# Causal mask and position bias added by VectorE inside the row maximum, in place of matmuls into the score bank

## The reference, cut to what matters

```
s_own = einsum('hqd,hld->hql', qi, k_own) * scale + table_t[:, rel_bucket(d_own)]
s_own = where(d_own[None] >= 0, s_own, -inf)
p = softmax(concatenate([s_sel, s_own], axis=-1))
```

## Time and profile before

| | before |
|---|---|
| median of three runs | 1194.9 us |
| profiled execution, first to last instruction | 1194.0 us |
| PE / DVE / ACT busy | 1178.5 / 742.4 / 623.6 us |
| score matmuls L1185 + L1189 | 96 + 96, of 128 to 512 columns |
| mask matmuls L1197 | 64 |
| bias matmuls L1494 | 64 |
| row maxima L2393 | 112, of them 96 in the three causal loops |

### The profile page before, as it was taken

How to read it: one execution, slowest core, us unless ns; L and a number is a source line. 1 busy time by engine, 2 the same in 40 slices (tenths; PEclk the granted TensorE clock), 3 DMA queues, 4 the chain that set the end, 5 groups by cost and what they waited for, 6 DMA issues and landing times.

```text
span 1194.0 us, 16132 instructions
## 1 busy us (share of the span) xinstructions
PE 1178.5 (99%) x6034; PEld 984.1 (82%) x6034; DVE 742.4 (62%) x1123; ACT 623.6 (52%) x1054; POOL 158.6 (13%) x255
## 2 busy tenths in 40 slices
PE   9999999999999999999999999999999999999997
PEld 7788887778888888888788898888898888888886
DVE  6667576755333475674387775455647659558478
ACT  5566785685332255532676554352455445464464
POOL 3233223410000021000133000010001010000010
PEclk9999999999999999999999999999999999999999
DMA  6422233113443543342112545221286553743732
GB/s 198 108 58 66 71 91 103 37 54 106 106 105 105 176 132 102 106 142 71 36 54 106 162 139 165 71 101 51 73 247 141 172 130 87 227 108 91 210 71 88
DMA packets 152139, 133.37 MB, mean 112 GB/s; under 512 B 5553, under 2 KB 124401, under 8 KB 152066
## 3 DMA queue, kind: packets, MB, share of 16 engines
q1 hardware_dynamic: 144688, 113.13, 31.6%
q0 software_dynamic: 4000, 13.67, 5.9%
q10 hardware_dynamic: 3378, 5.60, 1.5%
HBM read 115.55 MB, written 4.22 MB: 100 GB/s over the span
## 4 chain that ended last, share of the span: by engine, by line
PE 90%; DVE 5%; ACT 2%; DMA 1%; issue 1%; POOL 0%; DVEq 0%; ACTq 0%; POOLq 0%
PE lin L993 23%; PE lin L995 23%; PE lin L994 23%; PE tr L1175 2%; PE sc L994 2%; PE sc L995 2%; PE sc L993 2%; PE sc L1189 1%; PE sc L1185 1%; PE tr L1168 1%; PE tr L994 1%; PE tr L993 1%; PE tr L995 1%; DVE w_lo L2368 1%; PE lin L1213 1%
## 5 line engine op out<-in xcount | busy, mean ns | idle before, releaser
L993 PE MATMUL lin<-h_hi,w_hi 128*128 128x512 f32 (+1 forms) x824 | 318.0, 386 | 0.0
L995 PE MATMUL lin<-h_hi,w_lo 128*128 128x512 f32 (+1 forms) x824 | 310.5, 377 | 0.0
L994 PE MATMUL lin<-h_lo,w_hi 128*128 128x512 f32 (+1 forms) x824 | 310.4, 377 | 0.0
L2368 DVE TENSOR_TENSOR w_lo<-w_raw,w_hi 128x1024 fp32r<-128x1024 f32 x160 | 196.6, 1232 | 140.8 <-ACT w_hi L1637 139.7
L1637 ACT ACTIVATE w_hi<-w_raw 128x1024 fp32r<-128x1024 f32 x162 | 170.8, 1056 | 145.0 <-PE lin L995 48.6
L995 PEld LDWEIGHTS lin<-h_hi,w_lo 128*128 128x128 f32 x824 | 155.7, 189 | 28.5
L993 PEld LDWEIGHTS lin<-h_hi,w_hi 128*128 128x128 f32 x824 | 155.8, 189 | 27.2 <-issue 0.6
L994 PEld LDWEIGHTS lin<-h_lo,w_hi 128*128 128x128 f32 x824 | 156.1, 189 | 24.5
L2393 DVE TENSOR_REDUCE neg_max<-sc 128x1 f32<-128x128 f32 (+3 forms) x112 | 52.4, 478 | 55.4 <-PE sc L1189 35.5
L2368 DVE TENSOR_TENSOR u_lo<-u_raw,u_hi 128x256 fp32r<-128x256 f32 (+2 forms) x48 | 37.4, 779 | 68.6 <-ACT u_hi L2252 37.4
L993 PE MATMUL lin<-w_hi,h_hi 128*128 128x512 f32 x160 | 63.4, 397 | 0.0
(11 more groups left out here) (399 smaller groups left out, 2356.6 us busy)
## 6 DMA issues: line engine op xcount, KB each, us to landing
w_raw<-in_w_in SPq DMA_DIRECT2D x74, 512.0 KB, 3.9
w_raw<-in_w_up SPq DMA_DIRECT2D x32, 512.0 KB, 4.4
wd_b<-in_w_down SPq DMA_DIRECT2D x24, 512.0 KB, 5.3
w_raw<-in_w_out SPq DMA_DIRECT2D x16, 512.0 KB, 3.6
w_raw<-in_w_xkv SPq DMA_DIRECT2D x16, 512.0 KB, 3.9
x_m<-in_x SPq DMA_DIRECT2D x8, 512.0 KB, 5.6
w_raw<-in_w_branch SPq DMA_DIRECT2D x8, 512.0 KB, 4.2
w_raw<-in_w_xq SPq DMA_DIRECT2D x8, 512.0 KB, 3.9
```

Source lines behind the costliest of these rows:

```text
L993: pe.matmul(o, lh, rh, start=start, stop=False)
L994: pe.matmul(o, lh, rl, start=False, stop=False)
L995: return pe.matmul(o, ll, rh, start=False, stop=stop)
L2368: return dve.tensor_tensor(out, x, as_f32(hi), ALU.subtract)
```

## The change

For the 96 score tiles of fox, diff and moba, the mask and bias matmuls are gone. In place of the row maximum stands one `tensor_tensor_reduce` on DVE (`biased_max`): it reads the score bank and a bias tile in SBUF, writes -(score + bias) back over the bank, and takes the minimum of that, which is the negated maximum. The exponential reads the bank with scale -1. In fox and diff the bias tile is `bias_c`, zero with -1e30 above the diagonal in its last 128 columns, made by POOL behind the roots of the first norm; in moba there is one tile of 128x512 for each head. The bias rows are no longer split: 8 rows of 640 entries are written to memory 128 times each (8 x 128 x 640 floats, 2.6 MB, from 8 partitions), and read back with a row step of 639 entries into 8 tiles of 128x512 (2.1 MB, as many bytes as before). DVE, and no longer PE, waits for them. The warm-up matmuls at the start read ones in place of `ident_b` and `future_b`. The row maxima of "x" stay as they were.

```diff
+BIAS_ROW = 640
...
-             ("g_x", [P, 2, T], F32), ("beta", [P, BIAS_COLS], F32), ("one_hot", [P, BIAS_COLS], F32),
-             ("beta_hi", [P, BIAS_COLS], F32R), ("beta_lo", [P, BIAS_COLS], F32R), ("beta_0", [P, 1], F32)],
+             ("g_x", [P, 2, T], F32), ("beta", [P, BIAS_ROW], F32), ("one_hot", [P, BIAS_COLS], F32),
+             ("beta_0", [P, 1], F32)],
...
-            [("pad_z", [P, 34 * T], F32), ("bias_b", [P, 4 * 256], F32R)])
+            [("pad_z", [P, 34 * T], F32), ("bias_b", [P, 2 * T], F32)])
...
-            [("pad_b", [P, 4 * PT_COLS + P_COLS], F32), ("bias_a", [P, 9 * 256], F32R)],
+            [("pad_b", [P, 4 * PT_COLS + P_COLS], F32), ("bias_a", [P, 4 * T], F32)],
...
-        flip = sb("flip", [P, P], F32R)
...
-        bias_c = sb("bias_c", [P, 256], F32R)
-        ident_b = sb("ident_b", [P, P], BF16)
-        future_b = sb("future_b", [P, P], BF16)
+        bias_c = sb("bias_c", [P, T], F32)
...
-        bias_places = [B["bias_a"][:, :], B["bias_b"][:, :], c_row[:, :], bias_c[:, :]]
-        bias_16 = [place[:, 256 * n:256 * n + 256] for place in bias_places for n in range(place.shape[1] // 256)]
+        bias_places = [B["bias_a"][:, :], B["bias_b"][:, :], as_f32(c_row[:, :]), bias_c[:, :]]
+        bias_of = [place[:, T * n:T * n + T] for place in bias_places for n in range(place.shape[1] // T)]
...
-            for buf, value in ((ident[:, :], 0.0), (as_f32(ones_r[:, :]), 1.0), (as_f32(flip[:, :]), 0.0), (ident_b[:, :], 0.0),
-                               (future_b[:, :], 0.0), (minus_half[:, :], -0.5),
+            for buf, value in ((ident[:, :], 0.0), (as_f32(ones_r[:, :]), 1.0), (minus_half[:, :], -0.5),
                                (eps_n[:, 0:1], SUBLN_EPS), (eps_n[:, 1:2], EPS)):
                 link(pool.memset(buf, value))
-            for buf, sign, base in ((ident[:, :], -1, 0), (flip[:, :], 1, 1 - P), (ident_b[:, :], -1, 0)):
-                link(pool.affine_select(out=buf, in_=as_f32(buf) if buf.dtype == F32R else buf, compare_op=ALU.not_equal, fill=1.0,
-                                        base=base, pattern=[[sign, P]], channel_multiplier=1))
-            pool.affine_select(out=future_b[:, :], in_=future_b[:, :], compare_op=ALU.is_ge, fill=FAR, base=0,
+            pool.affine_select(out=ident[:, :], in_=ident[:, :], compare_op=ALU.not_equal, fill=1.0, base=0,
                                pattern=[[-1, P]], channel_multiplier=1).then_inc(consts_made, 1)
...
+            pool.memset(bias_c[:, :], 0.0).then_inc(mask_cleared, 1)
+            pool.wait_ge(mask_cleared, 1)
+            own_block = bias_c[:, T - P:T]
+            pool.affine_select(out=own_block, in_=own_block, compare_op=ALU.is_ge, fill=FAR, base=0,
+                               pattern=[[-1, P]], channel_multiplier=1).then_inc(mask_made, 1)
+            pool.wait_ge(mask_made, 1)
...
-            def stacked_scores(s, place, h, i, extra=None, q_rest=None):
+            def stacked_scores(s, place, h, i, q_rest=None):
...
-            def mask(o, i):
-                pe.matmul(o[:, P * i:P * i + P], ident_b[:, :], future_b[:, :], start=False, stop=False)
...
+            warm = ones[:, :].bitcast(BF16)[:, 0:P]
             for n in range(2 * WARM):
-                pe.matmul(lin[:, 3, 0:P], ident_b[:, :], future_b[:, :], start=True, stop=True)
+                pe.matmul(lin[:, 3, 0:P], warm, warm, start=True, stop=True)
...
-                stacked_scores(S0["fox"] + m, 0, h, i, lambda o, n: mask(o, i), B["q_one"][:, h % 2, P * i:P * i + P])
+                stacked_scores(S0["fox"] + m, 0, h, i, B["q_one"][:, h % 2, P * i:P * i + P])
...
                 for m in range(2):
-                    stacked_scores(S0["diff"] + 2 * w + m, 1, 2 * h + m, i, lambda o, n: mask(o, i))
+                    stacked_scores(S0["diff"] + 2 * w + m, 1, 2 * h + m, i)
...
-            pe.wait_ge(bias_in, 16 * 4)
...
-                near = max(i - 1, 0)
...
                     heads_ready("qa2", "ka2", h, 2)
-                def extra(o, n):
-                    for tile in (bias_16[h], bias_16[8 + h]):
-                        pe.matmul(o[:, P * near:n], flip[:, :], tile[:, 256 - (n - P * near):256],
-                                  start=False, stop=False)
-                stacked_scores(S0["moba"] + m, 2, h, i, extra)
+                stacked_scores(S0["moba"] + m, 2, h, i)
...
-            def exponentials(s, p, n):
+            def exponentials(s, p, n, sign=-1.0):
                 act.wait_ge(s_max, s + 1)
-                act.activation(p, sc[:, s % 2, 0:n], ACT.Exp, bias=neg_max[:, s:s + 1],
+                act.activation(p, sc[:, s % 2, 0:n], ACT.Exp, bias=neg_max[:, s:s + 1], scale=sign,
                                accum_out=denom[:, s:s + 1]).then_inc(s_exp, 1)
...
                 act.wait_ge(beta_ready, 1)
-                act.dma_start(bias_dram[0:8, :], as_f32(B["beta_hi"][0:8, :])).then_inc(beta_out, 16)
-                act.dma_start(bias_dram[8:16, :], as_f32(B["beta_lo"][0:8, :])).then_inc(beta_out, 16)
+                rows = B["beta"][0:8, :].rearrange("p (o r) -> p o r", o=1).to_broadcast([8, P, BIAS_ROW])
+                act.dma_start(bias_dram[:, :, :], rows).then_inc(beta_out, 16)
...
             def bias_tiles_in():
-                act.wait_ge(beta_out, 32)
-                with nc.allow_non_contiguous_dma(reason="overlapping rows: entry (p, c) is distance entry 1 + p + c"):
-                    first = 0
-                    for place in bias_places:
-                        n = place.shape[1] // 256
-                        src = bass.AP(bias_dram.tensor, first * BIAS_COLS + 1, [[1, P], [BIAS_COLS, n], [1, 256]])
-                        act.dma_start(as_f32(place).rearrange("p (h c) -> p h c", h=n), src).then_inc(bias_in, 16)
-                        first += n
+                act.wait_ge(beta_out, 16)
+                first = 0
+                for place in bias_places:
+                    n = place.shape[1] // T
+                    src = bass.AP(bias_dram.tensor, first * P * BIAS_ROW + P,
+                                  [[BIAS_ROW - 1, P], [P * BIAS_ROW, n], [1, T]])
+                    act.dma_start(place.rearrange("p (h c) -> p h c", h=n), src).then_inc(bias_in, 16)
+                    first += n
...
-                exponentials(S0["x"] + m, B["xp"][:, m % 4, :], MEM)
+                exponentials(S0["x"] + m, B["xp"][:, m % 4, :], MEM, 1.0)
...
+            def biased_max(s, n, bias):
+                dve.wait_ge(s_done, s + 1)
+                o = sc[:, s % 2, 0:n]
+                dve.tensor_tensor_reduce(o, o, bias[:, T - n:T], -1.0, 3.0e38, ALU.add, ALU.min,
+                                         neg_max[:, s:s + 1]).then_inc(s_max, 1)
...
-            def causal_max(name):
-                return lambda m: row_max(S0[name] + m, P * (m % 4 + 1))
+            def causal_max(name, bias):
+                return lambda m: biased_max(S0[name] + m, P * (m % 4 + 1), bias(m // 4))
...
-            attention("fox", 32, causal_max("fox"), fox_lo,
+            dve.wait_ge(mask_made, 1)
+            attention("fox", 32, causal_max("fox", lambda h: bias_c), fox_lo,
...
                 for m in range(2):
-                    row_max(S0["diff"] + 2 * w + m, P * (w % 4 + 1))
+                    biased_max(S0["diff"] + 2 * w + m, P * (w % 4 + 1), bias_c)
...
                 step(g)
+                far = BIAS_ROW - BIAS_COLS
                 link(dve.tensor_copy(B["beta_0"][0:8, 0:1], lin[0:8, g % 4, 0:1]))
-                dve.tensor_scalar(B["beta"][0:8, :], lin[0:8, g % 4, 0:BIAS_COLS], B["beta_0"][0:8, 0:1], None,
-                                  ALU.subtract).then_inc(dve_evac, 1)
+                dve.memset(B["beta"][0:8, 0:far], 0.0)
+                dve.tensor_scalar(B["beta"][0:8, far:BIAS_ROW], lin[0:8, g % 4, 0:BIAS_COLS], B["beta_0"][0:8, 0:1],
+                                  None, ALU.subtract).then_inc(dve_evac, 1)
                 dve.wait_ge(dve_evac, DN[g])
-                link(dve.memset(B["beta"][0:8, 257:BIAS_COLS], FAR))
-                link(dve.tensor_copy(B["beta_hi"][0:8, :], B["beta"][0:8, :]))
-                lo_part(B["beta_lo"][0:8, :], B["beta"][0:8, :], B["beta_hi"][0:8, :]).then_inc(beta_ready, 1)
+                dve.memset(B["beta"][0:8, far + 257:BIAS_ROW], FAR).then_inc(beta_ready, 1)
...
-            attention("moba", 32, causal_max("moba"), moba_lo, lambda m: invert(S0["moba"] + m),
+            dve.wait_ge(bias_in, 16 * 4)
+            attention("moba", 32, causal_max("moba", lambda h: bias_of[h]), moba_lo, lambda m: invert(S0["moba"] + m),
...
-    tensors["bias_dram"] = nc.dram_tensor("bias_dram", (16, BIAS_COLS), F32, kind="Internal").ap()
+    tensors["bias_dram"] = nc.dram_tensor("bias_dram", (8, P, BIAS_ROW), F32, kind="Internal").ap()
```

More of the change, by code:

```diff
@@ L468, in two_blocks_kernel @@
         consts_made = sem("consts_made")
+        mask_cleared = sem("mask_cleared")
+        mask_made = sem("mask_made")
```

(5 more changed lines are left out.)

## The result

The changed kernel takes 1222.14 us (median of 4 runs, 1221.63 to 1222.54) against 1195.36 us of the kernel before on the same chip (1194.89 to 1195.92): a ratio of 1.0226, 95% interval 1.0212 to 1.0240. It is 27 us **slower**; forecast were 1186.5 us and 0.7% faster. The profiled execution has a span of 1219.9 us at a mean clock of 0.985.

The account below looks back on a forecast made before the run. PE was taken to bound the kernel (busy 99% of the span), except DVE in part of moba and latency in diff. Loop gains 3.5 + 2.4 + 4.7 - 22 d made 8.4 us, giving 1186.5 us; range 1183.5 to 1191.5.

Parts of the forecast that it names:

- the one on the store: New 2.6 MB store on ACT's queue, issued at 469.0 us: costs zero, with 23 us of cover before ACT's copy.
- slow end of 33 us: The store at 79 GB/s would land at 502 us, 10 us late, losing 4 to 5 us.
- The prediction's own sign of this: ACT's copy near 492 us on time; the prediction is wrong if PE waits after 492 us.
- Rival 3: The store is late and ACT holds PE up: 4.5 us lost, 1191.0 us; chance 0.07, a third of it slower.
- fox: Fox loop: PE never waits, DVE's extra work stays hidden, and all 3.5 us of the mask matmuls come off.
- diff: Diff loop: 10 of 16 turns latency-bound, 6 PE's; 2.4 us gained less 1.0 us for DVE, so 1.4 us.
- moba: Moba loop: bias matmuls go, but a DVE-bound stretch gains nothing; 4.7 us less DVE's excess, so 3.5 us.
- PE's idle time in moba: In the moba loop, PE's idle time would grow from 0.9 us to some 4.
- The excess d: Extra time of the new DVE instruction over a plain maximum: 0.10 us taken, bounds 0 and 0.49.
- the prediction's sum: Gain of the three loops together: 10.6 - 22 d us, 8.4 us with d = 0.10.
- Rival 1: The new DVE instruction runs at half rate (d = 0.49): about 3.8 us slower, 1198.7 us; chance 0.07.
- still not bind: In fox at d = 0.49, DVE would have 65.8 of 72.5 us and not set the pace.

Follow-up runs that it names:

- run 2: The kernel before plus a 2.6 MB store from partitions 0 to 7, 128 times each, nobody waiting until the kernel's end: 1230.33 us, ratio 1.0299.
- run 12: The kernel before plus the 2.6 MB store from partitions 0 to 7, issued at 489.7 us in place of 468.3: 1220.45 us, ratio 1.0213.
- run 11: The changed kernel with each head's bias row stored once (20 KB) and read backwards, five rounds: 1186.37 us, ratio 0.9932 against the kernel before.
- run 1: The changed kernel with each head's bias row stored once (20 KB) and read backwards, first measurement: 1187.88 us, ratio 0.9935 against the kernel before.
- run 10: The changed kernel with the 20 KB store, an addition and a plain negated maximum replacing the one DVE instruction: 1210.52 us, ratio 1.0128 against the kernel before.
- run 13: The kernel before plus the 2.6 MB store from 8 partitions 4 apart (0, 4, ... 28), 128 times each: 1195.87 us, ratio 1.0001.

## Why the prediction was wrong, point by point

**The step that failed** is the one on the store: "I take zero: the four stores ran beside each other", with a slow end of 33 us and 4 to 5 us lost. It failed twice.
- Its size. The store took 51.5 us. The 79 GB/s of the earlier trace rows is the rate of stores from 128 partitions on 16 engines. This one had 8 engines, and by the grouping above four of them behind each of two ways out of SBUF. That 8 partitions get 8 engines, which the prediction cited from the Trainium skill ("DMA: Bandwidth & Descriptors") and no row then showed, is what the trace has: the store kept 47% of the 16 busy.
- Its victim. The prediction set the store against its own waiter (ACT at 492 us, 23 us of cover) and never against the other traffic on the engines. The load issued at 472.9 us landed 41.7 us later. The prediction's own sign of this came: ACT's copy of the cross scores stands at 521.8 us and not near 492. Rival 3 had the store late and ACT hold PE up, but priced it at 4.5 us through ACT's wait; run 2 has nobody waiting and loses 35 us. By the table the loss at this place begins at 14 to 26 us of store and is some 13 to 16 us less than its duration; at the place of run 12 it is 26 us less.

The sum with that term measured: 1195.4 - 8 (the loops) + 33.1 (PE's wait) + 2.0 (ten matmuls at the low clock with starts 0.43 us apart in place of 0.23) = 1222.5, against 1222.1 measured.

**Right, with their sizes** (first to last exponential of a loop; forecast in brackets): fox -3.3 us (-3.5; PE waits once, 0.4 us), diff -1.0 (-1.4), moba -3.2 and 0.4 behind it (-3.5). PE's idle time in moba grew from 0.9 to 3.7 us (forecast some 4), its waits at the places named: scores behind an exponential. The whole is 8.1 us by run 11 (8.4), and 1186.4 us stand against the forecast of 1186.5 for what is now the version without that store. That they meet to 0.1 us is luck: run 1, the same program, gave 1187.9.

**The excess d** was taken as 0.10; it is 0.07 to 0.08 on the chain. Put into the prediction's sum, this makes diff -1.6 and moba -3.9 us, so these two terms were too large by 0.6 and 0.3 us, and the d that was taken hid a part of it. The second row exists, as the Trainium skill, "VectorE: DVE Perf Modes", section "Two Vector instructions with no wait between them", says of an operation that writes its accumulator out, but its 0.14 us lie beside its neighbours. Rival 1's rule, half rate, doesn't show: 694 ns for 512 columns against the 685 of a plain maximum. The Trainium skill, "Vector Engine (DVE) Microarchitecture Reference", section 7, names it for one form of instruction, `S2S2D2_STT` (a scalar_tensor_tensor), with both sources in SBUF, and the multiplication that the prediction held against it is not of that form. One that is (L2622 of the kernel before, fp32, 512 columns, without an accumulator) takes 737 ns, 1.1 times the 678 of the multiplication and not twice; with an accumulator no run here has it. Rival 1's price was wrong too: run 10 has a mean d of 0.53 (0.33 at 128 columns to 0.73 at 512, by the starts of the two instructions) and lost 24 us against run 11, where the sum gave rival 1 some 12. That DVE in fox would "still not bind" at 0.49 failed in it: fox lost all of its 3.3 us. So the sum held near d = 0.1, and its slope towards larger d was some half of the real one; diff alone grew by 10.5 us, 0.66 for each of its 16 turns.

**Two sums of the prediction don't close**, and neither decides anything: rival 1's 3 + 4 - 3.5 is 3.5 and not 3.8 us, and by its own chances "faster" adds up to 0.88 and "slower" to 0.09, where it has 0.87 and 0.07.

## What to carry to other kernels

Price a new DMA against every transfer that shares its engines, not only against whoever waits for it: here the loads behind it got nothing for 13 us on the shared engines and then one packet for each of its own. Before a store from few partitions, count its engines and how many of them draw on the same group of partitions; the same bytes cost 35 us from partitions 0 to 7 and nothing from 0, 4, ... 28. And ask whether the bytes are needed at all: an overlapping read of 20 KB made the 2.6 MB superfluous, and with it the change is 0.7% faster, as its loops promised.

## What the runs showed of the hardware that was not expected

- Two queues on the same DMA engines, once both are served, alternate packet by packet though their sizes differ: 396 of 2560 bytes beside 394 of 512 in 20 us, so the queue with the small packets got a sixth of the bytes. Before that the later queue got no packet there for some 13 us.
- A group of partitions gave, by the grouping above, some 2560 B x 4 / 0.376 us = 27 GB/s to the four DMA engines that read it. One engine alone got (2560 / 0.106) 24; whether the group or the engine limits it then, no run tells.
- A tensor_tensor_reduce that reads a bank and SBUF and writes the bank took 2% longer than a plain maximum over all widths in fox and moba and 5% in diff (at 512 columns 694, 694 and 716 ns against 686, 685 and 686), and reading its SBUF operand from last to first cost nothing (moba, 512 columns: 694 ns forwards in the change, 692 backwards in run 11).
- After 33 us without work PE ran ten matmuls at the lower clock, 1.2 GHz, before the clock came back; 2 us.
- Executions of one kernel on one chip spread by 2.4 to 3.3 us (the kernel before, beside run 13: 1194.27 to 1197.60). In the profile of run 1 the clock was 0.91 from 10 to 30 us and the first exponential of fox came at 65.7 us, in run 11 at 63.2, with the same program: a difference near 2 us needs rounds, not one profile.
